# Two-layer encoder trunk with grouped MoE on one core: four fixed experts instead of three, both first units picked by TensorE, row stores awaited by tile

## The reference

```python
for i in range(2):                       # layer 0: attention (MLA), layer 1: bidirectional RG-LRU
    sh1, sc1, g1, sh2, sc2, g2 = split(silu(c) @ w_ada[i] + b_ada[i])
    x = x + g1 * mixer_i(modulate(x, norm_mix[i], sh1, sc1))          # x: 512 tokens x 1024
    h = modulate(x, norm_ffn[i], sh2, sc2)
    scores = sigmoid(h @ w_router)                                    # 32 experts in 8 groups of 4
    # best group by the sum of its two best (scores + bias), then the two best experts in it
    idx, w = route(h)                                                 # w: scores, normalised over the two
    for each expert e: y_e = (silu(h_e @ w_g[e]) * (h_e @ w_u[e])) @ w_dn[e]   # h_e: its tokens
    x = x + g2 * (w[:, 0] * y[idx[:, 0]] + w[:, 1] * y[idx[:, 1]])
```

## Time and profile before

| | us |
|---|---|
| median of 3 runs | 1774.68 (1772.63 to 1778.27) |
| profiled execution | 1780.21 |
| its span, first to last instruction | 1778.5 |
| PE busy | 1386.1 (78%) |
| DVE busy | 702.8 (40%) |
| ACT busy | 319.3 (18%) |
| POOL busy | 298.7 (17%) |
| moved by DMA | 517.54 MB, mean 291 GB/s |

### The profile page before, as it was taken

One profiled execution on the slowest core, in us unless ns is written; L12 is line 12 of the kernel. 1 busy time (PEld: TensorE's weight loads), 2 busy tenths in 40 slices (PEclk: granted clock), 3 DMA queues, 4 the chain that ended last, 5 costly groups with the idle time before them and its releaser, 6 DMA issues.

```text
span 1778.5 us, 32975 instructions
## 1 busy us (share of the span) xinstructions
PE 1386.1 (78%) x14027; PEld 807.4 (45%) x14027; DVE 702.8 (40%) x1277; ACT 319.3 (18%) x675; POOL 298.7 (17%) x347
## 2 busy tenths in 40 slices
PE   3998999967885866998654999795787668699753
PEld 2643555435552433575422444344454334376431
DVE  5675777655221111122103299874421111122112
ACT  3344555120000000011002233312010000011000
POOL 1001111000321122223100111100222112223200
PEclk9998999998987988999876999896998888899986
DMA  9644222578799999999994222037499999999996
GB/s 368 250 166 165 72 96 82 166 295 367 299 392 405 406 387 394 411 387 401 424 381 190 63 80 72 0 149 324 171 403 391 412 405 378 410 378 400 421 428 251
DMA packets 66072, 517.54 MB, mean 291 GB/s; under 512 B 13468, under 2 KB 26293, under 8 KB 48266
## 3 DMA queue, kind: packets, MB, share of 16 engines
q1 hardware_dynamic: 50544, 493.77, 69.7%
q0 software_dynamic: 11232, 16.50, 2.8%
q10 hardware_dynamic: 4154, 5.18, 0.8%
HBM read 507.32 MB, written 22.04 MB: 298 GB/s over the span
## 4 chain that ended last, share of the span: by engine, by line
PE 50%; DMA 32%; DVE 11%; issue 3%; ACT 2%; SPq 1%; another core or an unknown queue 1%; POOL 0%; POOLq 0%; DVEq 0%; ACTq 0%
DMA ring_gu<-in_moe_w_gu_dram 26%; PE ps L1116 15%; PE ps L1123 7%; PE ps L1052 3%; PE ps L819 3%; PE ps L952 3%; PE ps L1017 2%; DVE ring_dn L1885 2%; PE ps L972 2%; PE ps L863 2%; PE ps L926 2%; PE ps L1075 2%; DMA arena<-xn_dram,tok_idx 2%; PE ps L843 2%; PE ps L891 2%
## 5 line engine op out<-in xcount | busy, mean ns | idle before, releaser
L1116 PE MATMUL ps<-ring_gu,arena 128*32 128x256 f32 x5376 | 363.7, 415 | 141.0 <-DMA ring_gu<-in_moe_w_gu_dram 131.9
L1116 PEld LDWEIGHTS ps<-ring_gu,arena 128*32 128x32 f32 x5376 | 207.2, 119 | 272.6 <-DMA ring_gu<-in_moe_w_gu_dram 103.5
L1936 DVE TENSOR_TENSOR arena<-arena,ps 128x128 f32<-128x128 f32 x120 | 34.5, 288 | 689.8 <-ACT arena L1490 689.8
L678 POOL DMA_INDIRECT ys_dram<-arena,out_idx x120 | 119.1, 993 | 714.7 <-DVE arena L1930 698.6
L1123 PE MATMUL ps<-ring_dn,arena 128*32 128x256 f32 x2688 | 188.3, 384 | 21.4 <-issue 15.3
L1116 PE MATMUL ps<-arena 128*32 128x256 f32 x2304 | 151.3, 412 | 66.5 <-DMA arena<-in_moe_w_gu_dram 63.3
L1490 ACT ACTIVATE arena<-ps 128x128 f32<-128x128 f32 x120 | 33.3, 277 | 922.3 <-PE ps L1116 783.7
L671 POOL DMA_INDIRECT arena<-xn_dram,tok_idx x112 | 103.2, 921 | 300.5 <-DVE out_idx L2083 260.2
L1116 PEld LDWEIGHTS ps<-arena 128*32 128x32 f32 x2304 | 91.2, 118 | 117.5 <-DMA arena<-in_moe_w_gu_dram 42.3
L1123 PEld LDWEIGHTS ps<-ring_dn,arena 128*32 128x32 f32 x2688 | 107.0, 111 | 82.5 <-issue 35.8
L1017 PE MATMUL ps<-arena 128*128 128x512 f32 x256 | 110.6, 592 | 0.9 <-ACT arena L1244 0.9
(11 more groups left out here) (345 smaller groups left out, 1534.0 us busy)
## 6 DMA issues: line engine op xcount, KB each, us to landing
ring_gu<-in_moe_w_gu_dram SPq DMA_DIRECT2D x44, 4096.0 KB
ring_dn<-in_moe_w_dn_dram SPq DMA_DIRECT2D x44, 2048.0 KB
arena<-in_moe_w_gu_dram SPq DMA_DIRECT2D x20, 4096.0 KB
arena<-in_moe_w_dn_dram SPq DMA_DIRECT2D x20, 2048.0 KB
ring_gu<-in_w_ada_dram SPq DMA_DIRECT2D x12, 2048.0 KB, 20.4
ring_gu<-in_w_ada_dram SPq DMA_DIRECT2D x48, 512.0 KB, 4.7
arena<-in_rnn_w_in_dram SPq DMA_DIRECT2D x8, 1024.0 KB, 6.5
ring_dn<-ys_dram SPq DMA_DIRECT2D x8, 1024.0 KB, 7.9
```

The source lines that it names most:

```text
L678: g.indirect_dma_start(ys_dram, bass.IndirectOffsetOnAxis(ap=out_idx[:, col:col + 1], axis=0), yo[:, n % 4, :], None, bounds_check=2 * TIL ...
L1116: last = mm(ps[s_ * ROWS:(s_ + 1) * ROWS, pb, 0:2 * QF].rearrange("p (a b) -> p a b", a=2), rows[:, k, :], pair[:, :, s_, :], start=(k == ...
```

## The change

Four experts are fixed (`FIXED = 4`), so unit 1 is experts 2 and 3. Both units 0 and 1 now get their rows from PE: the one-hot matrix is the stationary operand and `x_tok` streams through with 512 columns (`pick_rows`), ACT or DVE copies the 128 x 512 result out of PSUM, and PE transposes it (`picks_transposed`). Unit 1 has no gather any more; the first gather is that of unit 2. The store of each row tile has a semaphore of its own, and each writer into that buffer waits for the tile it overwrites. The slot one-hots carry the token number and the routing weight side by side, so that one set of 226-column products gives both. The sums for the extra blocks move behind block 5. Down weights of the first expert and half of expert 2's gate/up weights are loaded earlier: in layer 0 inside the stream of stage rows, in layer 1 as soon as the mixer's last block is done.

```diff
-TRIPLE = 8
-FIXED = 3
-CAP = [2, 2, 2, 5, 4, 3, 3, 3] + [2] * (HEAVY - TRIPLE) + [1] * (NE - HEAVY)
+TRIPLE = 9
+FIXED = 4
+CAP = [2, 2, 2, 2, 5, 4, 3, 3, 3] + [2] * (HEAVY - TRIPLE) + [1] * (NE - HEAVY)
...
@@ sync engine
                             ch = 3 * (r // KT) + j
+                            if r == KT + 1 and j == 0:
+                                sp.wait_ge(S["o_done"], H // 2)
+                                sp.dma_start(DN[0].rearrange("p k n -> p (k n)"), dn_rows(l, 0)).then_inc(S["dn_in0"], 16)
+                                sp.dma_start(gu_halves[0], gu_rows(l, 2)[:, 0:KT * HALF]).then_inc(S["gu_in2"], 16)
                             sp.dma_start(stage[:, j, :], w_ada_v[1][:, r % KT, ch * D:(ch + 1) * D]
...
@@ GpSimd
-                pool.wait_ge(S["xn_saved"], 16 * TT * (l + 1))
+                for i in range(TT):
+                    pool.wait_ge(S[f"xn_saved{i}"], 16 * (l + 1))
                 pool.wait_ge(S["slots_ready"], l + 1)
...
-                gather(1)
+                gather(2)
...
@@ TensorE
+                def pick_rows(t, hf):
+                    g = STAGES[f"picks{l}_{t}"] + hf
+                    pe.wait_ge(*emptied(before_in_bank(g)))
+                    for i in range(TT):
+                        pe.wait_ge(S["picks_ready"], 2 * TT * l + TT * t + i + 1)
+                        last = mm(bank(g), picked_hot[t][:, i, :], x_tok[:, i, hf * HALF:(hf + 1) * HALF],
+                                  start=(i == 0), stop=(i == TT - 1))
+                    last.then_inc(S["unit"], 1)
...
+                for hf in range(2):
+                    pick_rows(0, hf)
                 for n in range(2):
                     pe.wait_ge(*emptied(STAGES[f"logits{l}_{n}"]))
-                pe.wait_ge(S["hot01_ready"], TT * (l + 1))
-                for k in range(KT):
-                    for i in range(TT):
-                        last = mm(ps[:, k // 4, (k % 4) * P:(k % 4 + 1) * P], x_tok[:, i, chunk(1, k)], hot01[:, i, :],
-                                  start=(i == 0), stop=(i == TT - 1))
-                last.then_inc(S["xT_made"], 1)
+                picks_transposed(0)
+                pick_rows(1, 0)
...
                 for n in range(NB):
                     if n == 2:
                         block_down(n - 1)
+                    if n == 3:
                         slots_products()
                     if n == TILES:
                         block_down(n - 1)
-                        rows_transposed(1)
+                        picks_transposed(1)
...
                     gate_up(2 + n % 2, mine_rows, GU[place % RING], range(KT // 2, KT)).then_inc(S["gu_done"], 1)
+                    if n == 1:
+                        pick_rows(1, 1)
...
@@ ScalarE
+                act.wait_ge(S["xn_saved1"], 16 * (l + 1))
+                picks_out(0, 0)
+                act.wait_ge(S["xn_saved2"], 16 * (l + 1))
                 rows_out(0)
+                picks_out(1, 0)
...
@@ VectorE
-                dve.wait_ge(S["xn_saved"], 16 * TT * (l + 1))
                 then(v.tensor_tensor(as_quad(masked), quad, in_group, ALU.mult))
                 then(v.tensor_tensor(as_quad(masked), as_quad(masked), out_group, ALU.add))
+                dve.wait_ge(S["xn_saved0"], 16 * (l + 1))
...
+                picks_hot(1)
+                dve.wait_ge(S["xn_saved3"], 16 * (l + 1))
                 then(v.tensor_tensor(ahead, key.rearrange("p (o e) -> p o e", o=1).to_broadcast([P, NE, NE]),
                                      key.rearrange("p (e o) -> p e o", o=1).to_broadcast([P, NE, NE]), ALU.is_gt))
                 then(v.tensor_reduce(order, ahead, AX.X, ALU.add))
+                dve.wait_ge(S["xn_saved1"], 16 * (l + 1))
+                g = STAGES[f"picks{l}_0"] + 1
+                dve.wait_ge(S["unit"], g + 1)
+                v.tensor_copy(picked_rows[0][:, HALF:2 * HALF], bank(g)).then_inc(S["d_free"], 1)
```

211 lines of the change are left out of this document (114 added, 97 removed).

## The result

| | kernel before | changed kernel | ratio (95% interval) |
|---|---|---|---|
| first comparison | 1773.95 us (4 runs) | 1754.46 us (4 runs, 1753.17 to 1757.93) | 0.9889 [0.9874, 0.9904] |
| third group of experiments, later | 1781.3 (9 runs) | 1752.62 (5 runs) | 0.9834 [0.9813, 0.9855] |

Faster by 1.1% and 1.7%. The forecast was 1740 for the median and 34.8 us less in the profile; measured were 19.5 and 28.7 us less. I worked with two profiles of the changed kernel, its first (execution 1757.9 us, span 1756.2) and that of the third group (span 1749.1), since they differ in something that the prediction rests on.

A forecast was written before the change was run, and what follows sets the result against it. Bound by the weight stream, so the gain is place 5's earlier end in each layer: 19.3 + 15.5 = 34.8, 1780.2 - 34.8 = 1745.4, 1740 us for the median; 8 in 10 from 1728 to 1757.

The forecast's parts named there:

- Step 1, the store waits: Layer 1's expert choice: DVE waits only for tile 0's store, not the last row store, and goes on 6.94 us earlier.
- Steps 2 and 3, picking: Layer 1 after the choice: unit 0's 16 picking instructions take 9.3 us; first gate/up starts 10.0 us earlier, at 1240.8.
- Steps 4 and 5, places 3 and 4: Layer 1's gate/up weight loads: place 3 issued at 1247.9, place 4 17.1 us later at 1265.0, 22.5 earlier than before.
- Step 6, the pauses: Layer 1: PE pauses during the first gather cost 5.1 us, all behind place 4's issue; place 5 issued at 1283.8.
- The forecast -19.3 for layer 1: Layer 1: place 5's load ends at 1299.5 instead of 1318.8; -22.5 with no pauses, -14.2 with them twice.
- Layer 0, the size of the stage delay: Layer 0's projection: a stage row is 10.4 us late behind 4.19 MB of early loads, PE and all behind it +5.7.
- earlier loads by themselves are worth nothing, DMA idles there: Start of the experts: saving DMA time by loading earlier gains nothing, since DMA idles ahead of the dense stream.
- -21.2 + 5.7 = -15.5: Layer 0: place 5's end 21.2 us earlier by the same chain as layer 1, less 5.7 for the stage-row delay.
- Later places keep their distance: Dense stream, both layers: with bytes the same, what place 5's end gains is kept by all later places.
- wrong if the dense stretch grows: Stream: stays 458 us at 402 GB/s; the prediction is wrong if the dense stretch grows.
- "stream rate" rival ("slower"): Dense stream: its rate falls, perhaps from expert 3's loads in another order; 4.0% eats the 34.8, 6% gives 1792. Chance 0.04.
- The base: Profiled execution of 1780.2 us, 5.5 above the median of 1774.7; so 1745.4 in the profile became 1740 for the median.

The follow-up runs named there:

- third group: Last of three groups of follow-up runs, each on a chip of its own; the kernel before took 1781.3 us there, the changed kernel 1752.62 us.
- experiment 1: Kernel before with only the store waits split: a semaphore for each row store, DVE waiting tile by tile; 1760.92 us, ratio 0.9926.
- first group: First of three groups of follow-up runs, each on a chip of its own; the kernel before took 1774.21 us there.
- experiment 2: Changed kernel without layer 0's early loads (first expert's down weights, half of expert 2's gate/up at their old places); 1750.37 us, ratio 0.9858.
- experiment 6: Changed kernel with layer 0's early loads issued behind the last stage row, ahead of the wait for the projection's end; 1747.72 us, ratio 0.9824.
- experiment 9: Experiment 6's kernel with further PE products, result overwritten, ahead of PE's wait for the expert choice in both layers; 1743.84 us, ratio 0.9788.
- experiment 4: Changed kernel with 24 more picking instructions (10.3 us at full clock) ahead of unit 1's second half in each layer; 1771.29 us.
- experiment 8: Changed kernel with the gathers of units 7 to 14 left out in both layers, those blocks using old rows; 1713.54 us, ratio 0.9628.
- experiment 12: Changed kernel with the scatters of blocks 28 to 59 of layer 1 writing no row, their instructions kept; 1746.73 us.
- experiment 10: Experiment 9's kernel with unit 1's first picking half moved from ahead of block 0's to behind block 1's gate/up; 1754.31 us, ratio 0.9825.

## Why the prediction came out as it did

**Step 1, the store waits: right.** No wait in either layer; alone it is worth 13.3 us of 14.1 (experiment 1), two thirds of the first comparison's 19.5.

**Steps 2 and 3, picking: right.** 10.09 and 8.50 us in the first profile, 8.60 and 8.57 in the third group, against 9.3; the clock came back later or earlier than assumed. First gate/up after the choice: 23.1 and 21.6, forecast 22.9.

**Steps 4 and 5, places 3 and 4: right where PE doesn't pause.** 17.7 us apart, forecast 17.1; slot products 3.33, forecast 3.0; no wait for one-hots. On the third group 20.6.

**Step 6, the pauses: right in size, wrong in cause.** The prediction had them come with the first gather, 5.1 us, all of it behind place 4's issue. Where they occur, places 3 and 5 are issued 6.0 us further apart, 2.9 of it ahead of place 4. In the first profile the gathers ran (1259.49 to 1264.2) beside PE and nothing paused; on the third group the pauses put place 5's issue 65.7 us after the choice (65.9 forecast). They belong to the group. And in this layer they didn't matter: without them place 5 was issued 61.2 after the choice and was in 20.3 us later, with them 65.7 and 15.7 later, 81.5 both times (81.6 forecast). In layer 0 the same way takes 80.8 us without pauses and 83.1 with them. The forecast -19.3 for layer 1 is met to 0.1, in the first profile by two errors that cancel: no pauses, and a queue that hadn't finished place 4.

The Trainium skill ("Runtime: NRT & Kernel Launch", Instruction fetch mechanics) says that the cost of crossing a block of instructions is mostly hidden. The profiles of the first group, with no pause, agree with it; whether the pauses of the others are instruction fetches no run shows.

**Layer 0, the size of the stage delay: this step failed.** The forecast +5.7 is PE's wait for the residual, and as such it was right: PE waits 5.51 us, behind one wait of 10.17 us on DVE (10.4 forecast as the lateness of the row). What the sum left out is the clock. Behind that wait the granted clock is 0.50 from 349.4 to 356.2, in experiment 2 it stays at 1.00; eight transposes take 1.97 us instead of 1.05 and the next 32 instructions 14.79 instead of 13.90. So the projection lost 7.5 us. Behind it another spell at 0.50 (397.2 to 404.0) meets the router's products, and the group choice comes 77.8 us after the attention's end in both profiles of the changed kernel, 69.2 before: **8.6 instead of 5.7**. The Trainium skill ("DMA: Bandwidth & Descriptors", Queues, rings and completion order) has each DMA engine take a queue's descriptors in ring order; the trace agrees, with a wait of 10.17 us for a row behind 4.19 MB.

**Layer 0, "earlier loads by themselves are worth nothing, DMA idles there": wrong, and hidden by luck.** From the group choice to place 5 in, it takes 80.8 and 83.1 us in the two profiles, against 102.7 before: -21.9 and -19.6, forecast -21.2. But without the early bytes it takes 87.9 (experiment 2), so the chain alone gives -14.8. Behind the projection the queue is short of time, not idle: the early bytes are worth 5.9 us from SP's first load on, and place 5 came 21.2 and 18.5 us after its issue, not 15.65. The term was -21.2 + 5.7 = -15.5 and came out at -13.2 and -10.9. For layer 1 no run tried the same. With both effects known the better place for the loads follows (experiments 6 and 9).

**"Later places keep their distance": nearly.** Moving the start by 10.3 us moved the end by 8.4 a layer (experiment 4). In the first profile the dense stretches were 2.4 and 1.8 us longer, in the third group 1.1 and 0.6 shorter, with the same program. By the prediction's own sign (wrong if the dense stretch grows) the first profile speaks against it and the third group's does not. The row traffic in the stretches (the indirect queue) was 0.2 MB a layer more than before in the first profile and 0.1 more in the third group; at experiment 8's 8.8 us per MB this is +1.8 and +0.9. It would fit the first profile and not the third group's, and it was not tried alone, so the cause stays open. The "stream rate" rival ("slower") named the order of the loads; that order is the same in both profiles, so it does not explain their difference.

**The base.** The profile of before is of an execution with pauses (1780.2). The 5.5 us that I took off to reach the median is about what such a group costs the kernel before (5 to 7) and not the changed one, as far as its one group tells; taking it off again for the changed kernel was then wrong. 1780.2 - 34.8 = 1745.4 stood against 1750.9 for a like execution and 1752.6 to 1754.5 for medians, 1740 against these. The measured medians lie in the range, at its upper end.

## What to carry to other kernels

In a kernel that streams weights, read when the queue becomes dense and by what chain, and then add up bytes as well: a load that is issued early is worth what the queue lacks later, and costs what stands behind it, the slower clock after the wait included, so put it behind the last small load that somebody waits for. Price small indirect transfers inside a dense stream by leaving some out: here 0.8% of the bytes held 2.1% of the time. And take a second profile of the kernel before from another group of runs before building on its pauses.

## What the runs showed of the hardware that was not expected

- Gathers of 4 KB rows inside a dense stream, instructions and rows together, cost 8.8 us per MB, 2.4 us for a unit's four instructions (experiment 8); scatters of such rows 1.7 us per MB in the stretch (experiment 12). Bytes alone are 2.5 us per MB at 402 GB/s.
- PE's issue pauses (mostly 0.33 or 0.8 us, 21 to 39 of them) are there in all profiles of a group of runs or in none (groups 1 to 3).
- One wait of 5.51 us of PE cost 1.8 us more behind it: the granted clock was 0.50 for 6.8 us (first profile against experiment 2).
- PE's granted clock fell back to 0.50 after 2.78 us without work although it had come back in between (experiment 9), and 1.98 us of idle cost 1.7 us in the next 128 instructions (experiment 10).
